# Sampled attention of a hybrid decoder step: seven places for selected pages, programs written out per sequence, first pages asked for during prompt attention

## The chip, the cores and the metric

The kernel runs on one core of a Trainium2 chip. The metric is device time in microseconds (us), lower is better. Engines are called TensorE (PE in rows; its weight loads PEld), VectorE (DVE), ScalarE (ACT), GpSimd (POOL) and SyncE (SP). SyncE computes nothing here: it reads page numbers and issues DMAs.

## The reference, cut to what matters

One layer runs for a prompt of 256 tokens and for 8 sampled sequences of 8 new tokens each, with 2048 tokens behind each. The change lies in the sampled sequences' attention. Each has 16 pages of 128 tokens in two caches; a page row holds the keys and values of 4 heads (512 numbers, so a page is 256 KB). `page_table` says which pages are a sequence's own.

```
past_c = pool_cmp[layer, page_table].reshape(DB, nbp, BLOCK, 2, N_KV, HEAD_DIM)
summ   = compress(past_c, w_cmp)                 # 32 blocks of 64 tokens, weighted sums of keys and values
s_c = einsum('bqghd,bngd->bqghn', qg, kc) * scale     # scores of the block sums
p_c = masked_softmax(s_c, ...);  o_c = p_c @ vc
imp = sum of p_c over the heads of a group            # importance of a block
top = top_k(imp, 15) and the current block
s_s = scores of q against the keys of the chosen blocks; softmax; o_s
s_w = scores against the last 512 tokens (cache_kv_win) and the new ones; softmax; o_w
o   = g0 * o_c + g1 * o_s + g2 * o_w
```

The kernel doesn't gather the chosen blocks. It loads all 16 selected-cache pages of a sequence and adds a mask (0 or -1e30) to the scores, made from the ranks of the 32 importances.

## The kernel before, in words

The stages are `load_and_norm`, `project_qkv`, `prompt_setup`, `prompt_attention`, `sample_attention`, then the projections, the recurrence, the merge and the feed-forward part. Each is one or more blocks: in a block each engine has a program of its own, the programs meet through semaphores only, and all engines meet at the block's end. SBUF regions are shared out by hand: `ring_attention` (`ringflat`), `work`, `xT` (whose contents are kept in memory during attention, as `x_kept`) and so on.

`prompt_attention` (L728 to L925) uses `ringflat` from its start for its own tiles. SyncE has no program in it and stands at the block's end.

`sample_attention` (L929) handles the 8 sequences one after the other. On TensorE, ScalarE, VectorE and SyncE a hardware loop (`Fori`) has the first seven (SyncE: six), and the last is written out after it; on GpSimd the loop has all eight. In a loop the value that an engine waits for is computed from the loop's register.

Places for pages, each of four pages (`slot`): `s0` to `s3` for the selected pages, `c0` to `c3` for the pages to be summed, `w` for the window (512 tokens). `s0` to `s3`, `w` and `c0` lie in `ringflat`, `c1` to `c3` in `work`.

One sequence `b` on each engine, in its order:
- GpSimd (L1034 to L1042): for each of `c0` to `c3`, wait for its pages and multiply them with the weights `wcmp` (L1040, 4 instructions each), steps `m0` to `m3`.
- TensorE, `turn` (L1057): `ktrans` (L1062) transposes the keys of a place, 8 transposes into two banks: `k0`, `k1`, `k2`, `k3`, `kw`; between them L1082 (`kc`) and `score` (L1069) for the block sums (`sc`) and for each place (`s0` to `s3`, `sw`); L1090, L1091 turn the block probabilities (`imp`). Then `block_sums(b + 1)` (L1054, 16 matmuls that sum what GpSimd multiplied; the last raises `summed`), the transposes of the probabilities (`tp`, L1120), the products with the values (`pv0` to `pv3`, L1128, straight from the same places; `pvw`, L1152 to L1160, for new tokens and window) and the last transpose (`fin`, L1167).
- ScalarE copies what TensorE transposed (L1191, L1192), takes the exponentials (L1206, L1208), copies the sums (L1181) and the result (L1225).
- VectorE, `turn` (L1239): from `sc` the maximum and the probabilities (L1243 to L1247, steps `cmax`, `pc`), then from `imp` (L1249) the ranks: L1252 to L1255 work on 128 x 1024 elements (32 x 32 comparisons), L1256 sums, L1257 makes the mask (`bias`). Only then are the scores of each place taken out of their bank with the mask added (L1263, `s0` to `s3`), the maximum found (L1267), and the window's likewise. The score of `s2` reuses the bank of `s0`, so it waits for `s0`'s add. At the end L1280 to L1282 make the output (`o`), which `fin` waits for.

What sets the order of the pages is SyncE's program (L976 to L1028). `load` reads four page numbers from `table` into registers (L982) and issues four DMAs (L984). `turn(b)` is: wait until the sums of `b + 1` are done (`summed`), then ask for `c0` and `c1` of `b + 2`; wait for `pv0` of `b`, ask for `s0` of `b + 1`; wait for `pv1`, ask for `s1`; `c2` of `b + 2`; wait for `pv2`, ask for `s2`; `c3`; wait for `pv3`, `s3`; wait for `pvw`, then `load_rest`: the window of `b + 1` (L988) and the new rows (L989, L990). `settled` (L263) raises a semaphore that nobody waits for. Before the loop come all pages of sequence 0, in the order summed, selected, window, and, when the first sums are done, the summed pages of sequence 1.

Of the kernel before, what the change touches and what calls it, by code (L numbers as in the profile page):

```python
# [23 lines left out]
T = 256  # L24
# [222 lines left out]
def _layer(nc, a, o, top):  # L247
# [479 lines left out]

    def prompt_attention():  # L728
        v = Carve(ringflat)
# [21 lines left out]
        with nc.Block() as block:  # L751
            @block.tensor
# [176 lines left out]
    def sample_attention():  # L929
# [16 lines left out]
        more = [v3(4, KVC) for _ in range(3)]  # L946
        slot = dict(s0=pages[0], s1=pages[1], s2=pages[2], s3=pages[3], w=pages[4], c0=pages[5], c1=more[0], c2=more[1], c3=more[2])
        landed = {n: sem(f"sa_landed_{n}") for n in slot}
# [19 lines left out]
        def arrived(eng, name, b):  # L968

            eng.wait_ge(landed[name], b * 64 + 64)  # L970
# [3 lines left out]
        with nc.Block() as block:  # L974
            @block.sync
            def _(sp):  # L976
                cmp_, sel_ = (a[n][0].rearrange("n t c g d -> n t (c g d)") for n in ("cache_kv_cmp", "cache_kv_sel"))

                def load(name, cache, b):
                    first = b * NPG + 4 * int(name[1])  # L980
                    numbers = table[0:1, ds(first, 4)].bitcast(I32)
                    _, four = nc.values_load_multi_w_load_instructions(numbers, engines=[mybir.EngineType.SP], min_val=0, max_val=cache.shape[0] - 1)  # L982
                    for j in range(4):
                        sp.dma_start(slot[name][:, j:j + 1, :], cache[ds(four[j], 1), :, :].rearrange("n t c -> t n c")).then_inc(landed[name], 16)  # L984

                def load_rest(b):
                    for j in range(4):
                        sp.dma_start(slot["w"][:, j:j + 1, :], a["cache_kv_win"][0, ds(b, 1), j * P:(j + 1) * P].rearrange("b t c g d -> t b (c g d)")).then_inc(landed["w"], 16)  # L988
                    sp.dma_start(vnew[0:TS, 0:1, :], o["kv_sel_sample"][0, ds(b, 1), :, 1].rearrange("b t g d -> t b (g d)")).then_inc(v_in, 16)  # L989
                    sp.dma_start(vnew[0:TS, 1:2, :], o["kv_win_sample"][0, ds(b, 1), WIN - TS:WIN, 1].rearrange("b t g d -> t b (g d)")).then_inc(v_in, 16)  # L990

                def summed_pages(qs, b):
                    for q in qs:
                        load(f"c{q}", cmp_, b)

                def selected_pages(q, b):
                    sp.wait_ge(PE.sem, PE.at(f"pv{q}", b))
                    settled(sp)
                    load(f"s{q}", sel_, b + 1)

                def turn(b, last_two):
                    if not last_two:
                        sp.wait_ge(summed, b * 1 + 2)
                        settled(sp)
                        summed_pages((0, 1), b + 2)
                    selected_pages(0, b)
                    selected_pages(1, b)
                    if not last_two:
                        summed_pages((2,), b + 2)
                    selected_pages(2, b)  # L1010
                    if not last_two:
                        summed_pages((3,), b + 2)
                    selected_pages(3, b)
                    sp.wait_ge(PE.sem, PE.at("pvw", b))
                    settled(sp)
                    load_rest(b + 1)

                summed_pages(Q, 0)
                for q in Q:
                    load(f"s{q}", sel_, 0)  # L1020
# [4 lines left out]
                with sp.Fori(0, LAST - 1) as b:  # L1025
                    turn(b, False)
# [1768 lines left out]
```

## Time and profile before

| | us |
|---|---|
| median of 3 runs | 3146.51 (3144.09 to 3147.22) |
| profiled execution | 3141.98 |
| its span, first to last instruction | 3140.1 |
| TensorE, VectorE, ScalarE, GpSimd busy | 2795.1, 1435.1, 955.6, 536.3 |
| mean granted clock of TensorE, share of full speed | 0.906 |
| DMA traffic over the span | 378.23 MB, 120 GB/s |

The shares are of the whole span, in which the stages have different limits; sampled attention is some 380 of the 3140 us. The profile's page also gives a chain of work that ended last, but it reaches back only to the start of the last stage. For this change one has to go to the stretches, the waits and the timeline of the stage itself.

### The profile page before, as it was taken

To read this page: it belongs to the slowest core of one execution; us is meant where nothing else is said; L and a number is where in the kernel's file an instruction comes from. 1 tells how busy PE (TensorE), PEld (TensorE's weight loads), DVE (VectorE), ACT (ScalarE), POOL (GpSimd) and SP (SyncE) were. 2 spreads that over 40 slices of the span, in tenths; PEclk is the share of its full clock that TensorE was granted. 3 is DMA by queue.
4 is the path that set the end of the run, shared out by engine and by line. 5 is a ranking of instruction groups with operands and counts; after the bars stand their busy time and mean duration, and the time that the engine had idled before them with its cause. 6 is when DMAs were issued, how large, how long until landed. Compare 5 with 4: busy or idle time off the path is not lost. (4 is left out here: it accounts for less than half of the span.)

```text
span 3140.1 us, 53620 instructions
## 1 busy us (share of the span) xinstructions
PE 2795.1 (89%) x19131; PEld 2364.2 (75%) x19131; DVE 1435.1 (46%) x2621; ACT 955.6 (30%) x1898; POOL 536.3 (17%) x616
## 2 busy tenths in 40 slices
PE   6898875676699699999999979898999999999999
PEld 4896653333499577777777747577999899999898
DVE  4542433444355355555555411006666643566633
ACT  3222322232333333333323210003444332344332
POOL 0000006545000143333334300000000000000000
PEclk9995556777799799999999989998999999999999
DMA  5730017557454122222222154423444354444353
GB/s 174 239 110 10 0 38 231 193 195 241 156 165 134 35 62 56 54 61 60 58 61 62 48 196 140 130 94 108 153 144 151 120 159 149 140 143 152 119 163 112
DMA packets 369288, 378.23 MB, mean 120 GB/s; under 512 B 37114, under 2 KB 329037, under 8 KB 367897
## 3 DMA queue, kind: packets, MB, share of 16 engines
q1 hardware_dynamic: 363444, 359.25, 38.0%
q0 software_dynamic: 1296, 13.11, 1.1%
q10 hardware_dynamic: 4438, 4.40, 0.5%
q8 instruction: 71, 1.16, 0.1%
q14 instruction: 39, 0.32, 0.0%
HBM read 357.00 MB, written 27.94 MB: 123 GB/s over the span
## 5 line engine op out<-in xcount | busy, mean ns | idle before, releaser
L229 DVE TENSOR_TENSOR ffn_lo<-ffn_raw,ffn_hi 128x1024 fp32r<-128x1024 f32 x264 | 319.6, 1223 | 365.9 <-ACT ffn_hi L225 365.6
L340 PE MATMUL bank<-n_hi,ffn_hi 128*128 128x320 f32 x1408 | 438.0, 311 | 14.9 <-DVE ffn_lo L229 14.9
L225 ACT CAST ffn_hi<-ffn_raw 128x1024 fp32r<-128x1024 f32 x264 | 275.7, 1049 | 557.1 <-PE bank L340 524.6
L340 PE MATMUL bank<-n_lo_ffn,ffn_hi 128*128 128x320 f32 x1408 | 436.8, 310 | 0.0
L340 PE MATMUL bank<-n_hi,ffn_lo 128*128 128x320 f32 x1408 | 436.6, 310 | 0.0
L340 PEld LDWEIGHTS bank<-n_hi,ffn_hi 128*128 128x128 f32 x1408 | 265.9, 189 | 16.2 <-issue 16.0
L340 PEld LDWEIGHTS bank<-n_lo_ffn,ffn_hi 128*128 128x128 f32 x1408 | 265.9, 189 | 0.0
L340 PEld LDWEIGHTS bank<-n_hi,ffn_lo 128*128 128x128 f32 x1408 | 265.9, 189 | 0.0
L340 PE MATMUL bank<-g_hi,ffn_hi 128*128 128x320 f32 x704 | 219.9, 312 | 13.5 <-DVE ffn_lo L229 13.5
L2030 POOL TENSOR_TENSOR gate_low<-work,gate_high 128x512 fp32r<-128x512 f32 x128 | 166.5, 1301 | 368.4 <-ACT gate_high L1912 368.4
L340 PE MATMUL bank<-g_lo,ffn_hi 128*128 128x320 f32 x704 | 218.9, 311 | 0.0
L340 PE MATMUL bank<-g_hi,ffn_lo 128*128 128x320 f32 x704 | 218.8, 311 | 0.0
L340 PE MATMUL bank<-n_hi,gate_high 128*128 128x320 f32 x512 | 188.3, 368 | 0.2
L340 PE MATMUL bank<-qkv_hi,n_hi 128*128 128x256 f32 (+3 forms) x528 | 152.0, 288 | 18.6 <-DVE qkv_lo L229 18.6
L340 PE MATMUL bank<-n_lo_shift,gate_high 128*128 128x320 f32 x512 | 158.3, 309 | 0.0
L340 PE MATMUL bank<-n_hi,gate_low 128*128 128x320 f32 x512 | 157.7, 308 | 0.0
L2563 POOL COPY ffn_work<-ffn_work 128x2 f32<-128x2 f32 x88 | 24.2, 275 | 779.7 <-ACT ffn_work L2534 542.0
L2354 PE MATMUL bank<-work,ring_out 128*128 128x320 f32 x512 | 139.6, 436 | 15.1 <-DMA ring_out<-w_out 15.1
L340 PE MATMUL bank<-qkv_lo,n_hi 128*128 128x256 f32 (+3 forms) x528 | 151.7, 288 | 0.0
L340 PE MATMUL bank<-qkv_hi,n_lo_qkv 128*128 128x256 f32 (+3 forms) x528 | 151.4, 287 | 0.0
L1040 POOL TENSOR_TENSOR work<-work 128x512 f32<-128x512 f32 x96 | 141.8, 1510 | 33.1 <-DMA work<-cache_kv_cmp 33.1
L340 PEld LDWEIGHTS bank<-g_hi,ffn_hi 128*128 128x128 f32 x704 | 133.5, 190 | 14.0 <-issue 14.0
(393 smaller groups left out, 5744.3 us busy)
## 6 DMA issues: line engine op xcount, KB each, us to landing
ffn_raw<-w_up SPq DMA_DIRECT2D x176, 512.0 KB, 3.7
ffn_raw<-w_down SPq DMA_DIRECT2D x88, 512.0 KB, 3.6
ring_attention<-cache_kv_sel SPq DMA_DIRECT2D x128, 256.0 KB, 3.6
work<-w_in SPq DMA_DIRECT2D x128, 256.0 KB, 2.8
work<-cache_kv_cmp SPq DMA_DIRECT2D x96, 256.0 KB, 3.6
shift_raw<-w_in SPq DMA_DIRECT2D x48, 512.0 KB, 3.7
qkv_raw<-w_in SPq DMA_DIRECT2D x40, 512.0 KB, 4.4
ring_out<-w_out SPq DMA_DIRECT2D x16, 1024.0 KB, 5.4
```

The lines of the kernel that those rows point to most:

```text
L225: self.nc.scalar.copy(self.hi[:, j % 4, :, 0:n], self.raw[:, j % 4, :, 0:n]).then_inc(self.rounded, 1)
L229: self.nc.vector.tensor_tensor(self.lo[:, j % 4, :, 0:n], self.raw[:, j % 4, :, 0:n], self.hi[:, j % 4, :, 0:n].bitcast(F32), ALU.subtract ...
L340: ins = nc.tensor.matmul(out, lhs, rhs, start=first and n == 0, stop=last and n == 2)
L1040: last = nc.gpsimd.tensor_tensor(x, x, wcmp.unsqueeze(2).to_broadcast([P, 2, NKV, HD]), ALU.mult)
L2030: nc.gpsimd.tensor_tensor(gate_low[n % 4][:, :, :], gate_raw[n % 4], gate_high[n % 4][:, :, :].bitcast(F32), ALU.subtract).then_inc(gate_c ...
L2354: last = nc.tensor.matmul(bank[g][:, 0:NT], slots[:, c, k, h * P:(h + 1) * P], mT[:, c % 2 * 8 + k, :], start=c % 2 == 0 and k == 0, stop= ...
L2563: nc.gpsimd.tensor_copy(dst[:, 0:2], ub[:, u, T:T + 2])
```

## The change

1. The selected pages have seven places (`sel_slot`), used by turns: group `q` of sequence `b` has place `(4 * b + q) % 7`, with a semaphore for each place. The places are `pages[0:4]`, `pages[5]`, one in `work`, and `qT`. `c0` and `c1` move to `xT`.
2. All engines' programs are written out for the 8 sequences, with no hardware loop; every waited-for value is a constant.
3. A SyncE program is added to the block of `prompt_attention`: it asks for `c0`, `c1`, all selected pages and the window of sequence 0. Prompt attention's own tiles move behind five page places.
4. SyncE's order: page numbers are read up to 16 at a time and ahead of the waits. `s0`, `s1`, `s2` of sequence `b + 2` are asked for after `pvw` of `b`; `s3` of `b + 1` after `pv0` of `b`; `c0` of `b + 2` after its sums, `c1` after `s3`, `c2` and `c3` after `pvw` and the window.

```diff
+    xT_rows = xT[:, :, :].rearrange("p a t -> p (a t)")
+    qT_rows = qT.rearrange("p a h t -> p (a h t)")
+    left = Carve(work, 448)
+    more = [page_rows(left(4 * KVC)) for _ in range(3)]
+    sel_slot = pages[0:4] + [pages[5], more[0], page_rows(qT_rows)]
+    slot = dict(w=pages[4], c0=page_rows(xT_rows[:, 0:2048]), c1=page_rows(xT_rows[:, 2048:4096]), c2=more[1], c3=more[2])
+    def page_numbers(first, n):
+        numbers = table[0:1, first:first + n].bitcast(I32)
+        return nc.values_load_multi_w_load_instructions(numbers, engines=[mybir.EngineType.SP], min_val=0, max_val=a["cache_kv_cmp"].shape[1] - 1)[1]
+    def load_selected(sp, i, four):
+        for j in range(4):
+            sp.dma_start(sel_slot[i % 7][:, j:j + 1, :], sel_[ds(four[j], 1), :, :].rearrange("n t c -> t n c")).then_inc(sel_landed[i % 7], 16)
...
     def prompt_attention():
-        v = Carve(ringflat)
+        v = Carve(ringflat, 5 * 2048)
...
+            @block.sync
+            def _(sp):
+                numbers = page_numbers(0, 8)
+                for q in range(2):
+                    load_summed(sp, q, numbers[4 * q:4 * q + 4])
+                for half in range(2):
+                    numbers = page_numbers(8 * half, 8)
+                    for q in range(2):
+                        load_selected(sp, 2 * half + q, numbers[4 * q:4 * q + 4])
+                load_window(sp, 0)
...
         def arrived(eng, name, b):
-            eng.wait_ge(landed[name], b * 64 + 64)
+            if name[0] == "s":
+                i = 4 * b + int(name[1])
+                eng.wait_ge(sel_landed[i % 7], i // 7 * 64 + 64)
+            else:
+                eng.wait_ge(landed[name], b * 64 + 64)
...
+                numbers = page_numbers(8, 8)
+                for q in (2, 3):
+                    load_summed(sp, q, numbers[4 * q - 8:4 * q - 4])
+                numbers = page_numbers(NPG, 12)
+                for i in (4, 5, 6):
+                    load_selected(sp, i, numbers[4 * i - 16:4 * i - 12])
+                new_rows(0)
+                numbers = page_numbers(NPG, 16)
+                sp.wait_ge(summed, 1)
+                settled(sp)
+                for q in Q:
+                    load_summed(sp, q, numbers[4 * q:4 * q + 4])
+                for b in range(LAST):
+                    after = b + 2 < DB
+                    if after:
+                        numbers = page_numbers((b + 2) * NPG, 16)
+                    fourth = page_numbers((b + 1) * NPG + 12, 4)
+                    if after:
+                        sp.wait_ge(summed, b + 2)
+                        settled(sp)
+                        load_summed(sp, 0, numbers[0:4])
+                    sp.wait_ge(PE.sem, PE.at("pv0", b))
+                    settled(sp)
+                    load_selected(sp, 4 * b + 7, fourth)
+                    if after:
+                        load_summed(sp, 1, numbers[4:8])
+                    sp.wait_ge(PE.sem, PE.at("pvw", b))
+                    settled(sp)
+                    load_window(sp, b + 1)
+                    new_rows(b + 1)
+                    if after:
+                        for q in (2, 3):
+                            load_summed(sp, q, numbers[4 * q:4 * q + 4])
+                        numbers = page_numbers((b + 2) * NPG, 12)
+                        for q in range(3):
+                            load_selected(sp, 4 * b + 8 + q, numbers[4 * q:4 * q + 4])
...
-                with pool.Fori(0, DB) as b:
+                for b in range(DB):
...
-                with pe.Fori(0, LAST) as b:
-                    turn(b, False)
-                turn(LAST, True)
+                for b in range(DB):
+                    turn(b, b == LAST)
```

`load_summed` and `load_window` are written like `load_selected`, for the places `c0` to `c3` and `w`; `new_rows` is the last two DMAs of the old `load_rest`. ScalarE's and VectorE's loops are written out in the same way as TensorE's.

## Rows read from the trace of the kernel before

**Rows 1.** Stretches: span, busy (count) PE PEld DVE ACT POOL, clock, DMA share, GB/s

```profile
275.80:457.00 181.20, 161.58 (x604) 121.51 (x604) 77.27 (x264) 61.28 (x196) 0.00 (x0) 0.51 0.00 0
457.00:487.00 30.00, 7.76 (x33) 0.81 (x32) 0.00 (x0) 0.50 (x2) 19.61 (x16) 0.50 0.78 256
487.00:529.80 42.80, 28.84 (x346) 16.52 (x342) 20.73 (x28) 13.73 (x28) 23.74 (x18) 0.81 0.57 188
529.80:803.00 273.20, 181.01 (x2053) 102.34 (x2053) 117.42 (x168) 80.38 (x174) 139.12 (x95) 0.74 0.62 204
```

**Rows 2.** Waits, 575 to 803 us: us in total, times, longest

```profile
PE bank L1062 <- DMA ring_attention<-cache_kv_sel: 63.0, 15, 6.3
```

**Rows 3.** Timeline of TensorE, 529 to 768 us: start, us, instructions [idle before <- what ended it]

```profile
534.74 1.54 PE L1062 MATMUL bank<-cst,ring_attention 128*128 128x128 f32 x6 [4.70 <-DMA ring_attention<-cache_kv_sel]
...
613.79 0.52 PE L1128 MATMUL bank<-ring_attention,work 128*32 128x64 f32 x24
...
627.33 1.97 PE L1062 MATMUL bank<-cst,ring_attention 128*128 128x128 f32 x8 [6.08 <-DMA ring_attention<-cache_kv_sel]
...
654.49 2.76 PE L1054 MATMUL bank<-work,cst 128*32 128x512 f32 x24
...
764.27 1.97 PE L1062 MATMUL bank<-cst,ring_attention 128*128 128x128 f32 x8 [5.89 <-DMA ring_attention<-cache_kv_sel]
```

**Rows 4.** Timeline of SyncE, 610 to 645 us

```profile
614.21 1.95 SPq L984 DMA_DIRECT2D ring_attention<-cache_kv_cmp  x4
617.79 1.88 SPq L984 DMA_DIRECT2D work<-cache_kv_cmp  x4
621.49 5.71 SPq L984 DMA_DIRECT2D ring_attention<-cache_kv_sel  x8
```

**Rows 5.** Timeline of VectorE, sequence 3

```profile
646.38 1.29 DVE L1263 TENSOR_TENSOR work<-bank,ring_attention 128x512 f32<-128x512 f32 x2
```

**Rows 6.** Lines L1040 and L982: ns min/median/max, first and last start in us

```profile
L1040 POOLq MODIFY_POOL_CONFIG  x16: 1/8/29, 461.3 to 740.0; - x16
...
L982 SPq TENSOR_LOAD <-work x64: 294/300/500, 457.8 to 807.8; - x64
```

**Rows 7.** Timeline of TensorE, sequence 0

```profile
490.59 1.09 PE L1062 MATMUL bank<-cst,ring_attention 128*128 128x128 f32 x8
...
517.76 1.93 PE L1054 MATMUL bank<-work,cst 128*32 128x512 f32 x8 [3.84 <-POOL work L1040]
```

**Rows 8.** Timeline of TensorE, sequence 7

```profile
804.09 1.97 PE L1062 MATMUL bank<-cst,ring_attention 128*128 128x128 f32 x8 [0.82 <-DMA ring_attention<-cache_kv_sel]
```

**Rows 9.** Timeline of TensorE, sequence 2

```profile
599.92 1.94 PE L1062 MATMUL bank<-cst,ring_attention 128*128 128x128 f32 x8 [4.72 <-DMA ring_attention<-cache_kv_sel]
```

**Rows 10.** Timeline of VectorE, sequence 2

```profile
599.91 1.29 DVE L1263 TENSOR_TENSOR work<-bank,ring_attention 128x512 f32<-128x512 f32 x2
```

**Rows 11.** Timeline of GpSimd, 619 to 650 us

```profile
619.47 4.92 POOL L1040 TENSOR_TENSOR ring_attention<-ring_attention,work 128x512 f32<-128x512 f32 x4 [17.25 <-DMA ring_attention<-cache_kv_cmp]
...
634.90 13.78 POOL L1040 TENSOR_TENSOR work<-work 128x512 f32<-128x512 f32 x8 [5.63 <-DMA work<-cache_kv_cmp]
```

**Rows 12.** Single lines of VectorE: ns min/median/max, first and last start

```profile
L1252 DVE TENSOR_TENSOR work<-ring_attention x8: 1224/1378/2143, 493.4 to 813.1; 128x1024 f32<-128x1024 f32 x8
...
L1247 DVE TENSOR_SCALAR ring_attention<-ring_attention x8: 285/286/289, 492.0 to 808.9; 128x128 f32<-128x128 f32 x8
...
L1257 DVE TENSOR_SCALAR ring_attention<-ring_attention x8: 181/1094/1102, 500.7 to 819.3; 128x32 f32<-128x32 f32 x8
...
L1277 DVE COPY ring_attention<-work x8: 169/169/3553, 514.2 to 831.5; 128x3 f32 x7, 128x3 f32<-128x3 f32 x1
```

**Rows 13.** Stretch of `project_qkv`, columns as rows 1

```profile
70.00:265.00 195.00, 183.49 (x1500) 183.00 (x1498) 85.09 (x120) 51.00 (x83) 1.79 (x4) 0.92 0.50 158
```

**Rows 14.** DMA queues, 70 to 265 us: packets, MB, share

```profile
q8 instruction: 12, 0.20, 0.4%
```

**Rows 15.** DMA issues: KB each, us to landing

```profile
work<-w_cmp SPq DMA_DIRECT2D x2, 32.0 KB, 2.3
```

More of the change, by code:

```diff
@@ L976, in _ @@
             def _(sp):
[L977 to L997, printed above, removed]
-                    settled(sp)
[L999 to L1013, printed above, removed]
+                def new_rows(b):
+                    sp.dma_start(vnew[0:TS, 0:1, :], o["kv_sel_sample"][0, b:b + 1, :, 1].rearrange("b t g d -> t b (g d)")).then_inc(v_in, 16)
+                    sp.dma_start(vnew[0:TS, 1:2, :], o["kv_win_sample"][0, b:b + 1, WIN - TS:WIN, 1].rearrange("b t g d -> t b (g d)")).then_inc(v_in, 16)
@@ L1014, in turn @@
                     sp.wait_ge(PE.sem, PE.at("pvw", b))
                     settled(sp)
[L1016 to L1020, printed above, removed]
-                load_rest(0)
-                sp.wait_ge(summed, 1)
-                settled(sp)
-                summed_pages(Q, 1)
-                with sp.Fori(0, LAST - 1) as b:
-                    turn(b, False)
-                turn(LAST - 1, True)
+                    load_window(sp, b + 1)
@@ L1107, in turn @@
                     score("s3", 4, lambda gp: Kq[:, 1, gp, :], 512)
-                    new = ds(b * TS + T, TS)
+                    new = slice(b * TS + T, b * TS + T + TS)
                     score_new("snew", 0, 0, 0)
@@ L1127, in pv @@
                             for g in range(NKV):
-                                last = mm(bank[6][group(g), 0:HD], keys[:, group(g)], slot[f"s{q}"][:, j, head_cols(g)], start=q == 0 and j == 0, stop=False)
+                                last = mm(bank[6][group(g), 0:HD], keys[:, group(g)], rows_of(f"s{q}", b)[:, j, head_cols(g)], start=q == 0 and j == 0, stop=False)
                         PE.done(f"pv{q}", last)
@@ L1185, in turn @@
                     act.wait_ge(PE.sem, PE.before(b))
-                    AC.done("q", nc.scalar.copy(qb.unsqueeze(1), qrows[:, ds(b, 1), :, :]))
+                    AC.done("q", nc.scalar.copy(qb.unsqueeze(1), qrows[:, b:b + 1, :, :]))
                     def keys(n):
@@ L1224, in turn @@
                         src = bank[0][0:HD, 128:256].rearrange("p (j e q) -> p j e q", e=2, q=TS)[:, :, e, :]
-                        AC.done(f"out{e}", nc.scalar.copy(oT[64 * e:64 * e + 64, :, ds(b * TS + T, TS)], src))
+                        AC.done(f"out{e}", nc.scalar.copy(oT[64 * e:64 * e + 64, :, b * TS + T:b * TS + T + TS], src))
                     AC.turn()
                 take_sums(0)
-                with act.Fori(0, LAST) as b:
-                    turn(b, False)
-                turn(LAST, True)
+                for b in range(DB):
+                    turn(b, b == LAST)
             @block.vector
@@ L1283, in turn @@
                     DV.turn()
-                with dve.Fori(0, LAST) as b:
-                    own.body(b, OWN2)
+                for b in range(DB):
                     turn(b)
-                own.end(LAST)
-                turn(LAST)
-    OWN2 = 17
     sample_attention()
```

21 lines of the change are left out of this document (15 added, 6 removed).

## The prediction

> **What bounds the kernel now.** The change touches one stage only, so I read from coarse to fine. The table of stretches [rows 1] puts sampled attention between 457 and 841 us: a start (457 to 487) in which TensorE does almost nothing, sequence 0, six sequences in 273.2 us (45.5 each), and sequence 7. Nothing is busy through: a sixth of the row of the six is TensorE 30, VectorE 20, GpSimd 23, ScalarE 13 us, and the DMA share is 0.62. So it is a chain of waits, and the reader is to look for who ends TensorE's idle time. The list of waits [rows 2] says: TensorE's key transposes (L1062) wait for selected pages.
>
> The timeline shows where. After a sequence's last transpose (`fin`, L1167) the first key transposes `k0` of the next start 4.70 to 6.31 us later, ended by a page's landing: 4.70 for sequence 1, 5.89 for sequence 6, 6.08 for sequence 3 [rows 3]; the six add up to 35.1 us. SyncE explains it [rows 4]: it can ask for `s0` only after `c0` and `c1` of two sequences ahead; the first of those goes out at 614.21, the first selected page at 621.49, after `fin`, while `pv0`, which frees the place, had ended at 614.31 [rows 3]. The later waits (`k2`, `k3`, about 3 us each) are mostly covered: the transposed keys are scored at once, but the add of the scores waits for the mask, and the mask comes out of a VectorE chain (L1243 to L1257) that starts from `k0`. In sequence 3 the first add begins at 646.38 [rows 5], `k3` had landed by 645.84. So one wait of three is on the path: `k0`.
>
> **The change, part by part.** The sum is made against the profiled execution (3141.98 us, span 3140.1); the median shown, 3146.51, is 4.5 above it.
>
> *First pages during prompt attention.* `c0`, `c1`, the sixteen selected pages and the window of sequence 0 are asked for in a stretch with no data traffic (0 GB/s, 180 us long) [rows 1]: 28 DMAs with their page numbers are some 21 us of SyncE, which has nothing else there, so no cost. GpSimd then need not wait until 465.53. It can't start at once: its semaphore clears last until 461.4 (first L1040 queue entry at 461.3) [rows 6]. 4.1 us gained; had the clears been free it would be 7.5. Of its four groups of 4.92 the third needs `c2`, asked for near 460.4 and landed by 466.4 (as `c0` took 5.94 from issue to use), used at 471.3.
>
> *Sequence 0.* The sums for sequence 1 wait for GpSimd, 3.84 us before the last quarter [rows 7]. GpSimd there starts 9.35 us after `k0`, since SyncE still had `load_rest` to issue. Now SyncE waits with its numbers read (its work from 457.8: 2.4+4.2+3.4+6.2+0.8+4.4 = 21.4 us, done 479.2, sums at about 483), so 6.0 after `k0`: 3.35 earlier. But then GpSimd runs beside all four of VectorE's wide operations instead of one, and both slow each other (below), some 2.2 us. I take 1.1; ends -1 and +4.
>
> *Seven places.* `s0` to `s2` are asked for a whole sequence ahead, `s3` once `pv0` is done. `k0` then follows `fin` with the gap that TensorE has between ready pieces, 0.1 us; the other end is the 0.82 before sequence 7's `k0`, where page and boundary can't be told apart [rows 8]. Gain 35.1 - 0.6 = 34.5; at 0.82 each, 30.2.
> The covered waits have a tail: in sequence 2 `k3`'s transposes end at 601.86, the add before them at 600.56, 1.3 us late [rows 9, 10]; in sequence 3 it is nothing. Over the six I take 0.7 each, 4.2 (0 to 7.8). Sequence 7: 0.8.
>
> *What is moved past what, on SyncE.* The window, the two new rows, `c2`, `c3` and twelve selected pages stand behind `pvw`. Four DMAs are 1.88 us, a group of four with its numbers 3.58 [rows 4], a list's read 0.3 of it [rows 6], so a number is some 0.3. After `pvw`: 2 + 0.8 + 4.2 + 3.4 + 6.2, then 5.8 for the next 20 numbers: 22.4 us, while the next sums are 31 later. The window lands 7 us after `pvw` and is wanted 28 later. `s1` to `s3`'s places are free at `pvw`. In all 29 of 40 us. Data: 204 GB/s over 45.5 us is 9.3 MB; over 40 us that is 232, and the start moved 256 at a share of 0.78 [rows 1]. Fits.
>
> *GpSimd's new times.* Count from the end of the sums, S (657.25 in sequence 3 [rows 3]; `fin` ends at S+8.9). `c0` is used at S+5.9, `c1` follows and ends at S+15.5, `c2` lands about S+16.5 and `c2`, `c3` run to about S+29.5, stretched; the next sums are wanted at S+35. Slack 5, so no wait there. But the cover changes: today `c0`, `c1` run inside the `k0` wait and only `c2`, `c3` meet VectorE's wide operations [rows 11]. These take 1.22 us alone and some 2.15 beside GpSimd; L1252 goes from 1.22 to 2.14 with a median of 1.38 (1.55 is the mean of the six), as GpSimd reaches it late [rows 12]. Now it is met in full: +0.6. L1247, on the same chain, has never been beside GpSimd (0.286); it will stand at about `fin`+5.4 with `c1` running to `fin`+6.6. Nearest rows: L1257 takes 0.18 alone and 1.09 beside it; L1277 0.17 alone and once 3.55 [rows 12]. Ends 0 and 3.4; I take L1257's 0.9 less a share for times when it misses, 0.8. Together +1.4 a sequence, +8.4; ends 0 and +24.
>
> This is the place where a page bears on the sum. The trace's 1.22 against 2.14 comes first [rows 12]; the Trainium skill ("SBUF — State Buffer", section "SBUF: two separate sides") says that VectorE and GpSimd share one port pair as an exclusive lock, taken by a GpSimd operation, by a VectorE one with two SBUF inputs, or by one in a two-port mode. L1247 has one input, so by that rule it waits only if it runs in such a mode; then the sum is as above, otherwise 4.8 us lower. No row of before decides it.
>
> *Programs written out.* What a loop's end costs on TensorE lies inside today's `k0` wait and goes with it: in the 34.5 already. Waits with fixed numbers: nothing. Code to read grows; the rival below has it. Cover: the projection, straight-line code too, has TensorE busy 183.5 of 195 us beside 12 instruction packets [rows 13, 14], and its idle time ended by other engines. Taken as 0.
>
> *Clock.* TensorE's granted clock is a mean 0.74 in the six [rows 1]; at the lower level (1.2 GHz) eight transposes take 1.97 us [rows 3], at the upper (2.4 GHz) 1.09 [rows 7]. With the idle 6 us gone `k0` might run at the upper one. Against it: sequence 7's `k0`, 0.82 after `fin`, still took 1.97 [rows 8]. Taken 0; the end is 0.9 us each for the transposes of `k0` and `k1`, both on the chain to the mask: 1.8 a sequence, 10.6.
>
> Sum: -4.1 - 1.1 - 34.5 - 4.2 - 0.8 + 8.4 = -36.3. Profile 3105.7, **median 3110**. A sequence in the middle takes 40.0 instead of 45.5. What is late next is VectorE's chain from `k0` to the mask. Later stages start earlier and else stay.
>
> **The rivals.**
> *The clock stays up* (0.15). For: TensorE no longer idles 6 us, and in sequence 0 it had the upper level for `k1` [rows 7]. Against: sequence 7. It adds two thirds of 10.6 and, with GpSimd then later against the chain, of the port's 8.4: 12.7, so 3097.
> *The port takes it* (0.12). GpSimd is in the chain's way longer: L1247 waits for a batch as L1277 did, or `c1` runs into L1252. 2.5 us more a sequence: 3125. Against: `c1` should end 1 us after L1247 starts.
> *A wait takes `k0`'s place* (0.06): `c2`, `c3`, behind `pvw` and in a burst of 6.3 MB, land late, GpSimd ends after S+35 and the sums wait, as in sequence 0. For the burst: it asks for 6.3 MB in 16.6 us, 380 GB/s, over anything seen. Against: `c2`, `c3` are ahead of the twelve selected pages. Half of the gain: 3128.
> *Instruction fetch* (0.04), the other side. Written out, each sequence's 684 matmuls and loads [rows 1] are, at 2998 for 12 packets [rows 13, 14], 2.7 packets, with waits 3. If TensorE stood for each: the nearest small load takes 2.3 us to land [rows 15], 21 packets, 48 us, against a gain of 36: 3158. It decides from 36.3/21 = 1.7 us each on. Against it: rows 13, and the loop's own first pass, freshly read, in which TensorE waited for GpSimd [rows 7] and for no code.
>
> **How the numbers follow.** Likeliest 0.63, 3110, its own range 3100 to 3119 (port 0 to 1.4 more, tail, gap). The 8 in 10 takes in the clock's case and the port's, 3096 to 3126; outside are the rest of the wait's and fetch's. A measurement of this kernel tells about 0.2% (6.3 us) from no change: faster by more needs a gain over 6.3, which all but fetch and a bad form of the wait give: 0.93; within 0.02; slower 0.05.
>
> **What would show it.** In the trace after: no idle before the first L1062 of a sequence; `fin` to `fin` 40.0; L1252 at 2.1 to 2.2 throughout, L1247 about 1.1; first GpSimd work 4 us after the stage's start; no wait of TensorE for GpSimd from sequence 1 on; granted clock near 0.74. Wrong if: L1062 still waits for pages (the order on SyncE), sums wait for L1040 (the wait's case), idle before TensorE's instructions that no engine released (fetch), or L1247 above 2 (the port).

## The result, and the profile after

The changed kernel took 3090.61 us (median of 4 runs, 3084.56 to 3096.27) against 3146.86 (3144.09 to 3149.03) for the kernel before: a ratio of 0.9821, 95% interval 0.9801 to 0.9842. The forecast was 3110 with a range of 3096 to 3126, so the direction was right and the gain of 56 us is half as large again as the forecast 36. The profiled execution took 3091.01 us (span 3089.2, granted clock 0.916) against 3141.98 (3140.1, 0.906).

Read in stages, everything lies in sampled attention: 383.4 us before, 327.4 after. The recurrence, which is not touched, took 758.1 and 762.9; over all the kernels of this study it lay between 758.0 and 766.4, and two that have the change but for one part took 758.0 and 758.2, so those 5 us do not come from the change. The other stages agree within 2 us.

The stretches of the changed kernel (span, busy (count) of PE, PEld, DVE, ACT and POOL, granted clock, DMA share, GB/s) are its start, sequence 0, the six sequences, and sequence 7; they answer to [rows 1]:

```profile
456.20:481.30 25.10, 7.70 (x33) 0.83 (x33) 0.00 (x0) 0.00 (x0) 19.61 (x16) 0.57 0.64 211
481.30:521.30 40.00, 26.55 (x347) 15.21 (x344) 19.82 (x28) 13.65 (x28) 25.16 (x18) 0.84 0.48 166
521.30:748.10 226.80, 157.60 (x2055) 90.84 (x2054) 120.36 (x168) 80.34 (x174) 138.85 (x95) 0.83 0.70 246
748.10:783.00 34.90, 25.06 (x310) 15.80 (x308) 15.48 (x28) 13.14 (x29) 0.00 (x0) 0.80 0.09 31
```

The six sequences fall from 273.2 to 226.8 us with the same number of instructions and the same bytes. Two columns are to be compared: the clock, 0.74 before and 0.83 now, and TensorE's busy time, 181.0 before and 157.6 now. TensorE does the same work in 23 us less. That is what the forecast, which had the clock near 0.74, did not have.

The waits of the six sequences (who waits for whom: us in total, times, longest). None of TensorE's is for a page; in place of [rows 2] stands VectorE's chain, which ends in the mask and the add of the scores:

```profile
PE bank L1102 <- DVE work L1294: 51.3, 6, 9.2
DVE ring_attention L1274 <- PE bank L1102: 19.1, 6, 4.0
```

TensorE's timeline around sequences 2 and 3 (start, us, instructions, [idle before <- what ended it]; L1095 was L1062, L1200 was L1167, L1087 was L1054, L1102 was L1069), to be held against [rows 3]:

```profile
511.43 1.07 PE L1087 MATMUL bank<-work,cst 128*32 128x512 f32 x8 [2.43 <-POOL work L1073]
512.42 1.09 PE L1153 MATMUL bank<-cst,work 128*128 128x128 f32 x8
...
521.25 1.91 PE L1095 MATMUL bank<-cst,ring_attention 128*128 128x128 f32 x8
...
597.46 0.27 PE L1200 MATMUL bank<-cst,work 128*64 128x128 f32 x1 [1.21 <-DVE work L1313]
597.57 1.03 PE L1095 MATMUL bank<-cst,work 128*128 128x128 f32 x8
600.24 1.97 PE L1095 MATMUL bank<-cst,work 128*128 128x128 f32 x8
...
616.95 1.93 PE L1102 MATMUL bank<-ring_attention,work 64*32 64x512 f32 x8 [8.18 <-DVE work L1294]
...
635.73 0.27 PE L1200 MATMUL bank<-cst,work 128*64 128x128 f32 x1 [1.21 <-DVE work L1313]
635.83 1.04 PE L1095 MATMUL bank<-cst,ring_attention 128*128 128x128 f32 x8
638.44 1.09 PE L1095 MATMUL bank<-cst,ring_attention 128*128 128x128 f32 x8
```

`k0` starts 0.1 us after `fin`: the wait is gone. And it takes 1.03 to 1.04 us where it took 1.97, the upper level of the clock (2.4 GHz) instead of the lower (1.2 GHz); in this profile `k0` is at the upper level from sequence 2 on. `k1` is only in two of the six (638.44 here, and 713.52); in the others it takes 1.97 as at 600.24, and the level rises again after it.

SyncE asks for the pages early enough. Its timeline in sequence 3 (L755 window, L747 summed pages, L751 selected pages), for [rows 4], and behind it the early requests:

```profile
290.77 11.66 SPq L751 DMA_DIRECT2D ring_attention<-cache_kv_sel  x16
...
596.37 2.62 SPq L755 DMA_DIRECT2D ring_attention<-cache_kv_win  x4
599.92 4.00 SPq L747 DMA_DIRECT2D work<-cache_kv_cmp  x8
608.15 6.16 SPq L751 DMA_DIRECT2D ring_attention<-cache_kv_sel  x12
627.33 1.90 SPq L747 DMA_DIRECT2D xT<-cache_kv_cmp  x4
629.48 1.88 SPq L751 DMA_DIRECT2D work<-cache_kv_sel  x4
```

GpSimd's timeline: the stage's first multiply at 459.74, 3.5 us after the stage's start, and in sequence 3 `c0`, `c1` and then `c2`, `c3` almost without a break, for [rows 11]:

```profile
459.74 9.82 POOL L1073 TENSOR_TENSOR xT<-xT,work 128x512 f32<-128x512 f32 x8 [191.69 <-issue]
...
601.03 4.95 POOL L1073 TENSOR_TENSOR xT<-xT,work 128x512 f32<-128x512 f32 x4 [0.76 <-DMA xT<-cache_kv_cmp]
606.21 13.51 POOL L1073 TENSOR_TENSOR work<-work 128x512 f32<-128x512 f32 x8 [0.23 <-DMA work<-cache_kv_cmp]
```

Single lines of VectorE (ns min/median/max, first and last start), for [rows 12]; L1283 was L1252, L1278 was L1247:

```profile
L1283 DVE TENSOR_TENSOR work<-ring_attention x8: 1225/1860/2236, 487.6 to 755.5; 128x1024 f32<-128x1024 f32 x8
L1278 DVE TENSOR_SCALAR ring_attention<-ring_attention x8: 287/289/1153, 486.0 to 751.8; 128x128 f32<-128x128 f32 x8
```

Where the time went, worked out from the two timelines (mean of sequences 1 to 6, us). `cmax` is the start of VectorE's first step in a sequence (L1274), `wide` the start of the first wide operation (L1283) and `mask` the mask's start (L1288):

```
segment              before  after   change   forecast
fin to k0 start        6.12   0.12    -6.0     -5.75
k0 to cmax             3.92   2.92    -1.0      0     (clock -0.8, programs written out -0.2)
cmax to wide           4.62   3.86    -0.76    +0.8   (clock; L1278's stretch is covered)
wide to mask           9.46   9.70    +0.24    +0.6   (GpSimd beside VectorE)
mask to next fin                      -0.22    -0.7   (tail)
fin to fin            45.54  37.79    -7.75    -5.05
```

L1278 stretched in two of the six, but that cost nothing. In sequence 3 it ends at 602.38, and the transposes behind it (L1123), which need its result, begin at 604.00, straight after TensorE's own work at the lower level and with no idle time before them:

```profile
601.46 0.92 DVE L1278 TENSOR_SCALAR ring_attention<-ring_attention 128x128 f32<-128x128 f32 x1
604.00 0.64 PE L1123 MATMUL bank<-ring_attention,cst 128*128 128x32 f32 x2
```

Start to first `k0`: 29.3 to 25.1 (-4.2, forecast -4.1). Sequence 0: 43.0 to 40.2 (-2.8, forecast -1.1). Sequence 7: 37.22 to 34.87 (-2.35, forecast -0.8).

### The profile page after: what moved, and what is told of

It reads as the page before. It is cut to its first block and busy times, and to the rows that moved or that the text cites. A ratio compares the mean times of both kernels' runs of the same rounds, so it can differ in the third digit from the quotient of the medians.

```text
span 3089.2 us, 52725 instructions
## 1 busy us (share of the span) xinstructions
PE 2770.8 (90%) x19131; PEld 2351.9 (76%) x19131; DVE 1438.2 (47%) x2621; ACT 955.0 (31%) x1898; POOL 536.4 (17%) x616
## 5 line engine op out<-in xcount | busy, mean ns | idle before, releaser
L2381 PEld LDWEIGHTS bank<-work,ring_out 128*128 128x128 f32 x512 | 98.8, 193 | 56.9 <-issue 17.3
```

What stands on the lines that cost most here:

```text
L2381: last = nc.tensor.matmul(bank[g][:, 0:NT], slots[:, c, k, h * P:(h + 1) * P], mT[:, c % 2 * 8 + k, :], start=c % 2 == 0 and k == 0, stop= ...
```

## The experiments

My theory after the result: (A) the places and the order take the wait away, as forecast, and because TensorE no longer idles for 6 us before `k0`, its clock is at the upper level for `k0` and `k1`, some 1.8 us a sequence and 11 in all. The rivals: (B) the programs written out give a part; (C) the early requests give more than the 5 us forecast; (D) GpSimd gets out of VectorE's way more than thought, not the clock. The last experiments ask what bounds the kernel now. Kernels are compared by their ratio to runs of the kernel before on the same chip; those were 3147.26, 3145.51 and 3144.19 us in the three groups that have several rounds.

**The programs written out alone** (the kernel before; 3149.01 us, ratio 1.0003, 0.9994 to 1.0013, 10 runs).

```diff
-                with pe.Fori(0, LAST) as b:
-                    turn(b, False)
-                turn(LAST, True)
+                for b in range(DB):
+                    turn(b, b == LAST)
```

> The kernel before with only the programs written out; four places, the old order of pages. Theory (the gain is the k0 wait of 6 us and the clock that it costs): k0 still waits about 6 us, k0 to the first VectorE step (cmax) still 3.9 us, sequences 44.5 to 45.5, time 3140 to 3148. Rival (writing out is itself worth the excess, by cheaper waits or code read in order): k0 to cmax 2.8, sequences about 43.5, 3130 to 3136. Rival (instruction reads): slower, above 3153.

It is worth nothing that can be measured. The gaps before `k0` stay, 4.6 to 7.9 us in sequences 1 to 6, and so does the lower level in `k0` (TensorE, sequence 4):

```profile
674.55 1.76 PE L1061 MATMUL bank<-cst,ring_attention 128*128 128x128 f32 x7 [7.94 <-DMA ring_attention<-cache_kv_sel]
```

(B) falls, as far as the whole time goes. So does the forecast's rival of instruction fetch: written out, the code has no loop to stay in, and no time is lost. Two small things do change. `k0` to `cmax`, expected at 3.9, is 3.73 in all six sequences; it was 3.92 in the loop's passes and 3.72 in sequence 7, which the kernel before has outside the loop. And the first add follows the mask after 0.04 us instead of 0.12. That is 0.27 a sequence, which is lost in the page wait here (the sequences take 43.8 to 47.4, expected 44.5 to 45.5); the changed kernel with its loops kept was not run.

**TensorE kept busy in the old wait** (the kernel above with ten plain matmuls ahead of `k0`; 3158.19 us, ratio 1.0031, 1.0016 to 1.0045, 8 runs).

```diff
+                    if b:
+                        for _ in range(10):
+                            mm(bank[5][:, :], ident, Kq[:, 0, 0, :], start=True, stop=True)
                     ktrans("k0", "s0")
```

> The same as e1 with ten 128x128 by 512 matmuls, whose result nobody reads, before k0 of sequences 1 to 7, so that TensorE is busy for some 4.7 us of the 6 us wait. Clock theory: TensorE stays at its upper level into k0; k0 to cmax falls from 3.9 to 2.8, cmax to the wide operations by some 0.8, a sequence 1 to 1.9 us shorter, 7 to 13 us faster than e1. Rival (k0 is quick in the changed kernel for another reason): no change, or up to 3 us a sequence slower where the fillers run at the lower level and overshoot the wait.

The TensorE timeline of sequence 4:

```profile
668.40 8.75 PE L1079 MATMUL bank<-ring_attention,cst 128*128 128x512 f32 x20
676.99 1.04 PE L1061 MATMUL bank<-cst,ring_attention 128*128 128x128 f32 x8
679.59 1.09 PE L1061 MATMUL bank<-cst,ring_attention 128*128 128x128 f32 x8
...
686.34 1.48 PE L1061 MATMUL bank<-cst,ring_attention 128*128 128x128 f32 x8 [4.19 <-DMA ring_attention<-cache_kv_sel]
```

The mechanism is confirmed from this side: with nothing changed but that TensorE has work in the wait, `k0` and `k1` take 1.04 and 1.09 in all six sequences, `k0` to `cmax` takes 2.73 instead of 3.73, and `cmax` to `wide` 2.70 instead of 4.8 to 5.2. The time, which I expected to fall, did not: it rose by 9 us. One cause is mine: the fillers take 8.75 us (10.44 in two of the sequences) and not the 4.7 that I had put in, so they outlast the wait, and `k0` starts 2.6 us later than without them. Behind the mask another 1.0 is lost, where the waits for `k2` and `k3` add up to 43 us instead of 34, the longest 5.5: with four places the next pages can be asked for only as places come free. So the 3.3 us a sequence that the clock gives are used up, and the mean of the six is 45.9 in both kernels. The stage's profile accounts for 1.6 of the 9 us only (389.5 against 387.9, sequence 7 being 3.3 longer); the rest lies outside this stage, the recurrence for one at 766.4 against 763.0, and no run says why.

**The wait put back into the changed kernel.** Three reductions of 2.3 us (in a second kernel one) on VectorE after the last result of a sequence, and `k0` waits for them; nothing else is changed.

```diff
+                    for n in range(3):
+                        own(nc.vector.tensor_reduce(small[:, 15:16], S, AX.X, ALU.max))
+                    dve.sem_inc(hold, 1)
...
+                    if b:
+                        pe.wait_ge(hold, b)
                     ktrans("k0", "s0")
```

> The changed kernel with three more reductions (6.9 us) on VectorE at a sequence's end, for which k0 of the next waits: an idle TensorE as the page wait was, without any page being late. Clock theory: k0 to cmax 3.7, cmax to wide 4.6 or more, granted clock of a sequence near 0.74, a sequence 6.4 us of wait plus 1.5 to 2 of clock longer: 45.8 to 46.3. Rival (the clock in the changed kernel is no consequence of the missing idle time): k0 to cmax stays 2.8, sequences 44.2.

> The same with one reduction (2.3 us), so k0 waits some 1.9 us. If a short idle time is enough to lose the upper level for k0, k0 to cmax is 3.7 here too and a sequence 3.5 to 4 us longer than 37.8; if it takes the long one, k0 to cmax stays 2.8 and a sequence is 1.9 longer.

Three reductions: one run, 3146.23 us. The changed kernel is back at the old time: 6.55 us of idle, sequences of 44.0 to 44.5, and sequence 7, which waits too, 44.4 instead of 34.9. One reduction: one run, 3115.99 us, sequences of 41.0 to 42.8, a mean of 41.4. TensorE's timeline, first with three, then with one:

```profile
615.91 1.97 PE L1096 MATMUL bank<-cst,work 128*128 128x128 f32 x8 [6.55 <-DVEq L1319]
619.52 1.97 PE L1096 MATMUL bank<-cst,work 128*128 128x128 f32 x8
```

```profile
607.12 1.70 PE L1096 MATMUL bank<-cst,work 128*128 128x128 f32 x8 [1.90 <-DVEq L1319]
...
610.45 1.97 PE L1096 MATMUL bank<-cst,work 128*128 128x128 f32 x8
```

With three reductions `k0` to `cmax` is 3.73 again, and `cmax` to `wide` 4.74: together 1.7 more than in the changed kernel. With one, `k0` takes 1.49 to 1.97 and `k1` 1.97 in all six, and a wait of 1.9 us (1.5 in sequence 5) costs 3.6 a sequence (3.0 against the repeated kernel below): about 1.6 beyond itself, 1.2 of it between `k0` and `wide`. That is (A) from the other side, and it says why the forecast's evidence misled: a gap far shorter than 6 us is already enough. With three reductions the sum is less than I expected (44.0 to 44.5, not 45.8 to 46.3): the later chain meets GpSimd less. From `wide` to the mask's end it is 9.3 us instead of 10.8, most of it in the mask itself, which takes 0.18 instead of 1.09. So a part of (D) is real, but with the opposite sign: taking the wait away brings VectorE more of GpSimd, not less.

**Four places and the old order, the early requests kept** (3142.53 us, ratio 0.9994, 0.9985 to 1.0003, 10 runs).

```diff
-            sp.dma_start(sel_slot[i % 7][:, j:j + 1, :], ...).then_inc(sel_landed[i % 7], 16)
+            sp.dma_start(sel_slot[i % 4][:, j:j + 1, :], ...).then_inc(sel_landed[i % 4], 16)
...
+                def selected(q, b):
+                    sp.wait_ge(PE.sem, PE.at(f"pv{q}", b))
+                    settled(sp)
+                    load_selected(sp, 4 * (b + 1) + q, page_numbers((b + 1) * NPG + 4 * q, 4))
```

> The changed kernel with four places and the old order of requests, but first pages asked for during prompt attention and programs written out. Theory (places and order carry the middle sequences, the early requests the start): k0 waits some 6 us again, sequences 1 to 6 take 45 to 47, the start and sequence 0 keep 4 and 3 us; 3139 to 3143. Rival (the early requests are worth the 17.7 us that e2 lost, whatever the order): 3130.

```profile
620.87 1.97 PE L1093 MATMUL bank<-cst,ring_attention 128*128 128x128 f32 x8 [5.93 <-DMA ring_attention<-cache_kv_sel]
```

The gaps before `k0` are back, 5.9 to 7.6 us, `k0` takes 1.97, the sequences 45.0 to 47.4. The places and the order carry the middle of the stage. The early requests do give the start and sequence 0 together, from the end of prompt attention to `fin`, 7.2 us in the profile (65.0 instead of 72.2), as in the changed kernel; but the six sequences behind them take 4.8 us and sequence 7 1.0 more than in the kernel before, so that over the whole kernel at most some 5 us (the interval) and perhaps nothing is left. Why is not shown; two profiles of the changed kernel differ by 3.8 in the same six.

**The changed kernel without the early requests, and the changed kernel again, on one chip** (3106.14 us, ratio 0.9872, 0.9855 to 0.9888; and 3088.46, ratio 0.9805, 0.9789 to 0.9822; 4 runs each).

```diff
-            @block.sync
-            def _(sp):
-                numbers = page_numbers(0, 8)
...
+                numbers = page_numbers(0, 16)
+                for q in range(4):
+                    load_selected(sp, q, numbers[4 * q:4 * q + 4])
+                load_window(sp, 0)
                 numbers = page_numbers(NPG, 12)
```

> The changed kernel without SyncE's program in prompt attention: the pages of sequence 0 are asked for at the start of sampled attention. Forecast of the prediction: 4.1 us at the start and 1.1 in sequence 0 are lost, so 5 us above the changed kernel. Rival (the whole excess of the start is from it): 9 us, the 5.8 seen at k0 of sequence 0 and the 2.9 in it. Rival (page requests of sequence 0 only shift the bottleneck to SyncE, which now reads 32 numbers and issues 28 DMAs first): 10 to 15 us, since c0 to c3 of sequence 1 come late too.

> The changed kernel again, for comparison on this chip. The stage of sampled attention should be 327 us long as in its first profile; if the recurrence (758 us before, 763 after) is longer by chance, it comes back to 758 here and the time to 3086; if the change causes it, it stays at 763.

The early requests are worth 17.7 us here, more than the 15 of the largest rival; the forecast had 5.2 for them (4.1 and 1.1). SyncE and TensorE of the kernel without them:

```profile
484.34 1.85 SPq L755 DMA_DIRECT2D ring_attention<-cache_kv_win  x4
...
502.94 4.05 SPq L747 DMA_DIRECT2D xT<-cache_kv_cmp  x8
```

```profile
514.05 1.93 PE L1082 MATMUL bank<-xT,cst 128*32 128x512 f32 x8 [3.90 <-POOL xT L1068]
...
528.65 1.94 PE L1082 MATMUL bank<-work,cst 128*32 128x512 f32 x8 [2.96 <-POOL work L1068]
```

In the new order SyncE asks, right after sequence 0's own pages, for three groups of sequence 1's selected pages. Without an early start all that comes before `c0` of sequence 1, which goes out at 502.94 only: TensorE waits for all four quarters of the sums, and sequence 0 takes 52.8 us instead of 40. Sequences 1 to 6 are as in the changed kernel (36.7 to 38.4). The start is 5.4 us longer than there. So the two parts are no sum of independent gains: start and sequence 0 take 83.5 us in the new order without the early requests, 72.2 in the kernel before, and 65.0 with them in either order. Against the kernel before: written out 0, places with their order -41, early requests on top of them -18.

The repeated kernel also shows the spread of one profile to another: its stage took 331.1, not 327.4, a sequence 38.4 in the mean and not 37.8, at a clock of 0.80 instead of 0.83. The missing gap does not bring the upper level every time. In sequences 1, 4 and 5 `k0` takes 1.76, 1.91 and 1.30; in sequence 4 the level had already fallen before `fin`, which took 0.39 instead of 0.27 after its wait of 1.21:

```profile
637.35 0.39 PE L1200 MATMUL bank<-cst,work 128*64 128x128 f32 x1 [1.21 <-DVE work L1313]
637.54 1.91 PE L1095 MATMUL bank<-cst,ring_attention 128*128 128x128 f32 x8
```

The recurrence took 763.7 here too, which I had put down as the sign that the change causes it. The two variants that speak against it are the kernel without early requests and the one without the multiply below, with 758.0 and 758.2.

**GpSimd almost out of the way** (3049.46 us, 3047.37 to 3051.58, ratio 0.9689, 0.9669 to 0.9708).

```diff
+                            x = x[:, :, :, 0:2]
-                            last = nc.gpsimd.tensor_tensor(x, x, wcmp.unsqueeze(2)..., ALU.mult)
+                            last = nc.gpsimd.tensor_tensor(x, x, wcmp[:, :, 0:2].unsqueeze(2)..., ALU.mult)
```

> The changed kernel with GpSimd's multiplication (L1073) cut to 2 of the 64 columns of each head; the rest of the summed pages is left unweighted. It takes GpSimd out of VectorE's way. Port theory: from the wide operations to the mask a sequence takes 6.3 us as sequence 7 does, instead of 9.7, and L1278 never stretches: 3.4 to 4 us less in each of sequences 1 to 6, some 3 in sequence 0 and about 5 before it (sums wait for pages only): 25 to 33 us faster than the changed kernel, 3056 to 3064. Rival (the prediction's own size: the port costs 1.4 a sequence more than before, and the rest of the chain hides it): 8 to 15 us.

It leaves 62 of the 64 columns of each head unweighted, so its results are not the reference's. By the ratios it is 36 us below the changed kernel, a little above what I expected. Ten of them are the stage's start, where the multiply itself is waited for; the sequences fall to 34.1. VectorE, six sequences (busy us, mean ns | idle before):

```profile
L1285 DVE TENSOR_TENSOR ring_attention<-ring_attention 128x1024 f32<-128x1024 f32 x6 | 7.3, 1224 | 0.2
...
L1279 DVE TENSOR_SCALAR ring_attention<-ring_attention 128x128 f32<-128x128 f32 x6 | 1.7, 289 | 0.2
```

Without GpSimd beside it every wide operation takes 1.22 to 1.23, and L1278 (L1279 here) never stretches. The other 26 us are what the two engines cost each other, with what follows from it for the later waits.

**One input of the wide comparisons from PSUM** (3078.15 us, ratio 0.9778, 0.9761 to 0.9796, 5 runs).

```diff
-                    each, other = imp.unsqueeze(2)..., imp.unsqueeze(1).to_broadcast([P, NBLK, NBLK])
+                    each, other = imp.unsqueeze(2)..., bank[7][:, 96:128].unsqueeze(1).to_broadcast([P, NBLK, NBLK])
```

> The changed kernel with one input of the two comparisons (L1283, L1284) read from TensorE's bank instead of its copy in SBUF. Port theory, in the form of the skill's rule (a VectorE operation with two SBUF inputs shares a port with GpSimd): the two take 1.2 to 1.3 us beside GpSimd as alone, not 2.1; 1.6 us a sequence, 10 to 12 in all, 3077 to 3080. Rival (GpSimd slows VectorE's SBUF traffic of any kind, or reading the bank is itself slower): both stay near 2.1, no change.

VectorE's lines in this kernel:

```profile
L1283 DVE TENSOR_TENSOR work<-bank,ring_attention x8: 1224/1224/1225, 490.2 to 744.1; 128x1024 f32<-128x1024 f32 x8
...
L1286 DVE TENSOR_TENSOR work<-work,ring_attention x8: 1226/2170/2176, 494.8 to 747.8; 128x1024 f32<-128x1024 f32 x8
```

The line with one operand in PSUM takes 1.22 in all eight sequences, though GpSimd is at work beside it; the sum three lines on, with both in SBUF, still takes 2.17. The stage falls to 315.2. The gain in the whole time is likely rather than shown: the interval overlaps that of the repeated changed kernel (0.9789 to 0.9822).

**The equality and its products in PSUM too, in halves** (one in bank 5, one in bank 0; 3070.02 us, ratio 0.9756, 0.9741 to 0.9771, 4 runs), **and then the ranks and the block probabilities** (3064.82 us, 3061.53 to 3064.86, ratio 0.9743, 0.9730 to 0.9756, 5 runs).

```diff
+                    for r, e in halves:
+                        own(tt(e, other[:, r, :], each[:, r, :], ALU.is_equal))
+                    for r, e in halves:
+                        own(tt(e, e, const("earlier", NBLK, NBLK)[:, r, :], ALU.mult))
+                    for r, e in halves:
+                        own(tt(gt[:, r, :], gt[:, r, :], e, ALU.add))
...
-                    own(nc.vector.tensor_reduce(rank, gt, AX.X, ALU.add))
+                    own(nc.vector.tensor_reduce(bank[7][:, 192:224], gt, AX.X, ALU.add))
```

> As e5, and the equality, its product and the sum kept in two of TensorE's banks (in halves, since a bank holds 512), so that no rank operation has two SBUF inputs. Port theory: none of them stretches beside GpSimd; L1252's successors take 1.2 + 3 x 1.3 = 5.1 us instead of e5's 6.3, a sequence 1 us shorter than e5, 3069 to 3073. Rival (reading and writing banks costs VectorE as much as the port did): 3076 to 3082.

> As e8, and the ranks and the block probabilities go through a bank as well, so that the two one-input VectorE operations that stretched (the mask, 0.18 to 1.09, and the probabilities, 0.29 to 1.3) read no SBUF. If these two wait for the port because both of their sides are in SBUF, they fall to 0.2 and 0.3 and a sequence to 34.5 or less, 3058 to 3064. Rival (they wait for something else, since their output stays in SBUF): they stay, 3069 to 3073 as e8.

VectorE's groups in the first of the two, then single lines of the second:

```profile
L1278 DVE TENSOR_SCALAR ring_attention<-ring_attention 128x128 f32<-128x128 f32 x8 | 5.0, 628 | 0.3
...
L1292 DVE TENSOR_SCALAR ring_attention<-ring_attention 128x32 f32<-128x32 f32 x8 | 6.4, 801 | 0.3
```

```profile
L1292 DVE TENSOR_SCALAR ring_attention<-bank x8: 191/191/192, 497.2 to 734.4; 128x32 f32<-128x32 f32 x8
...
L1278 DVE TENSOR_SCALAR ring_attention<-bank,ring_attention x8: 351/352/353, 486.6 to 725.9; 128x128 f32<-128x128 f32 x8
```

The two operations with one input, which take 0.18 and 0.29 us alone and had a mean of 0.80 and 0.63 in the first kernel, take 0.19 and 0.35 throughout once that input comes from PSUM. The whole is 5 us, 0.8 us short of the expected range; the intervals of the two kernels overlap, so the durations are shown and the gain of this last step is only likely. Together with the step before it this is the best version: it computes what the changed kernel computes, its stage takes 300.8 us and a sequence 33.2 to 34.7, 0.6 to 0.8 points below the changed kernel's two ratios and 2.6% below the kernel before.

## Why the forecast was 20 us short

**The step that failed is the clock**, "Taken 0; the end is 0.9 us each for the transposes of `k0` and `k1` ... 1.8 a sequence, 10.6". The mechanism and even its size were in the text, as a rival with a chance of 0.15. Measured, the two segments from `k0` to `wide` are 1.76 a sequence shorter; 0.19 of it came with the programs written out (3.92 to 3.73 above), so the clock is 1.6 a sequence, 9.4 in six, and the wait put back takes 1.7 of the same two segments away again. Of the 1.6 `k0` is about 0.8 (five of six at the upper level) and `k1` 0.3 (two of six); the rest lies in the matmuls between and behind them in the same segments, which I have not separated one by one. TensorE's busy time falls by more, 23 us, but much of that lies where it waits for VectorE's add afterwards, up to 9.2 us at a time. The clock also explains most of sequences 0 and 7. In sequence 0 TensorE now waits 2.43 instead of 3.84 for GpSimd ahead of the last sums, and these and the eight transposes behind them take 1.07 and 1.09, where they took 1.93 [rows 7] and 1.97; with the matmuls after them that is 2.3 of the 2.8 gained there. In sequence 7 it is some 1.4.

The argument against it was one row: sequence 7's `k0`, 0.82 us after `fin`, still took 1.97 [rows 8]. The row was read as "a short gap does not bring the upper level back". What I did not look at is what TensorE had done ahead of that gap: it was idle 1.23 us before `fin`, which still took 0.27, and 0.82 after it. In the changed kernel the same transition with 0.1 us has the upper level in most sequences; with 1.90 us put back it is lost again. So the row was one case with a gap, and was taken for the rule of cases without one. But `k0` was slow with no gap too, in sequence 1 of the changed kernel (1.91) and in three of six when it was repeated. So what a gap of 0.82 does is not settled by these runs; that one of 1.9 suffices is.

**The wait before `k0`: right.** Forecast 34.5, measured 36.0; it is 0.1 us at every boundary. The order on SyncE held: the window, the new rows and the groups went out in the time worked out from [rows 4], and no sums waited for GpSimd from sequence 1 on.

**VectorE beside GpSimd: right in kind, too large; this term is 7 of the 20 us.** Forecast +1.4 a sequence, measured +0.24 on the chain. L1283 rose from a mean of 1.55 to 1.95, not to 2.15, since GpSimd is not beside it for its whole length in each sequence. L1278 did stretch, which it never had before, but only in two of six sequences (1.15 and 0.92 us; in the repeated run in four, 0.84 to 1.32), and in both TensorE was at the lower level in `k1` and finished later than it, so it added nothing and not 0.8. The forecast had no such cover. Its stretched value was well judged by the neighbouring line L1288, its frequency and its place on the chain were not. The Trainium skill ("SBUF — State Buffer", section "SBUF: two separate sides") has the port pair taken by a VectorE operation with two SBUF inputs or by one in a two-port mode. For two inputs the runs agree: 2.17 with both in SBUF beside GpSimd, 1.22 with one moved to PSUM. For L1278 and L1288, with one input, they show the wait, and show it gone with that input in PSUM; by the page's rule these then ran in the two-port mode, which no row names.

**The tail: too large.** I took 0.7 a sequence for `k2` and `k3`, of which 0.22 came. The mask, not the last key, ends the chain: the add begins as soon as the mask is done, 1.1 us after its start, and the rest runs as before.

**The early requests: priced as if alone.** 5.2 forecast, 17.7 in this kernel, in the old order 7.2 at the start and over the whole kernel 0 to 5. The sum of the parts was not wrong by this, since the forecast was made for both together and SyncE's 21 us were counted as gone; but the text gave a reader no sign that without them the new order delays the next sequence's sums. And one slip: "a sequence in the middle takes 40.0" does not follow from the terms, which give 45.5 - 30.3/6 = 40.5. Measured: 37.8.

**What did not happen.** Instruction fetch: the written-out stage read 17 and 11 packets of code in the six sequences, and the written-out kernel alone has a ratio of 1.0003. A wait in `k0`'s place: none for pages or sums. The forecast's remark on it, that 380 GB/s were "over anything seen", was wrong by the kernel before itself, which moved 396 GB/s for 1.1 us in sequence 0 and 497 for 4.9 us in the projection; in the changed kernel's six sequences single stretches of 5.7 us reach 404.

The balance in the stage: 9.4 (clock) + 1.1 (programs written out) + 7.0 (port smaller, six times 1.16) + 1.5 (gap) - 2.9 (tail) = 16.1 for the six, and 1.7 and 1.6 for sequences 0 and 7: 19.4 of the 19.7 by which the stage's gain of 56.0 exceeds 36.3. So the clock alone does not make up the miss; without the port's term, which erred the same way, about a third of it would be gone.

## What to carry to other kernels

When a wait of TensorE is taken away, price what follows it at both levels of its clock, and look at what the engine did before each row that is used as evidence; one boundary is not a rule. When an order of requests is changed, price each part also as the only one: here one part cost 11 us at the stage's start that another took away with 7 more, and the sum hid it. And where VectorE and GpSimd share a stretch, an operand that already lies in PSUM is the cheap way out: reading it there, instead of from its copy in SBUF, took 1.22 us against up to 2.24. For one line of code the ratio went from 0.9805 (0.9821 in the first runs) to 0.9778, with intervals that overlap, and for all of these operations to 0.9743, clear of both.

## What the runs showed of the hardware

An idle time of 1.9 us on TensorE was enough for the eight transposes behind it to take 1.49 to 1.97 us instead of 1.03 to 1.05, and for the next eight to take 1.97 in six of six sequences instead of four. Without it the upper level was not certain: `k0` took 1.30 to 1.91 in one of six sequences of the first profile and in three of the second. Twenty matmul instructions that did nothing useful, in place of a wait of 4.6 to 7.9 us, kept the upper level through `k0` and `k1`, and won no time.

GpSimd's multiplies slow some VectorE operations with a single SBUF input as well: TENSOR_SCALAR on 128x128 from 0.29 to as much as 1.40 us, on 128x32 from 0.18 to 1.09. With that input in PSUM they take 0.35 and 0.19 and do not vary. The reduction that stands between the wide operations and the mask has one SBUF input too (128x1024) and takes 1.22 beside GpSimd as without it.
